# Splitting the sparse-attention indexer's logits into three runs between projection pairs

## What is computed

```python
h = a * jax.nn.sigmoid(gate)                                   # conv group
...
logits = jnp.einsum('bthd,bsd->bths', iqb, ik)                 # 8 indexer heads of width 64
score = jnp.einsum('bths,bth->bts', jax.nn.relu(logits), iwb)  # weighted sum over the heads
score = jnp.where(s_pos <= t_pos, score, -jnp.inf)             # causal
_, idx = lax.top_k(score, topk)                                # topk = 128
```

## Time and profile before

| what | us |
|---|---|
| median of 3 runs | 2079.93 (2078.42 to 2082.22) |
| the profiled execution's own time | 2080.25 |
| its span, from the first to the last instruction | 2078.5 |
| TensorE busy | 2041.9 (98% of the span) |
| VectorE busy | 1325.9 (64%) |
| ScalarE busy | 647.3 (31%) |
| GpSimd busy | 388.3 (19%) |
| mean granted TensorE clock | 0.995 |

### The profile page before, as it was taken

The page is one execution under the profiler, slowest core; times in us unless marked ns, Lnnn a source line. Parts: engine busy times, 40 slices in busy tenths (PEclk is TensorE's granted clock), DMA queues, the critical chain, the costliest instruction groups (busy, mean ns, idle before and its releaser), DMA issues.

```text
span 2078.5 us, 32707 instructions
## 1 busy us (share of the span) xinstructions
PE 2041.9 (98%) x12681; PEld 1813.2 (87%) x12681; DVE 1325.9 (64%) x1891; ACT 647.3 (31%) x1027; POOL 388.3 (19%) x187
## 2 busy tenths in 40 slices
PE   8999999999999899999999999999999999999997
PEld 7778888866888789898999989899998989999896
DVE  1069995364111877675757768576776857677688
ACT  2020000255000154252433425243342524334250
POOL 5536655234556310000000000000000000000010
PEclk9999999999999999999999999999999999999999
DMA  6323343401533234242442423344342333424242
GB/s 198 86 72 90 101 101 99 115 35 41 202 102 102 61 82 132 71 120 85 122 123 82 129 75 109 95 115 123 87 123 82 96 108 103 132 81 126 88 143 81
DMA packets 292039, 214.02 MB, mean 103 GB/s; under 512 B 9510, under 2 KB 256102, under 8 KB 289994
## 3 DMA queue, kind: packets, MB, share of 16 engines
q1 hardware_dynamic: 291834, 211.97, 34.8%
q10 hardware_dynamic: 80, 0.13, 0.0%
HBM read 207.76 MB, written 4.19 MB: 102 GB/s over the span
## 4 chain that ended last, share of the span: by engine, by line
PE 94%; DVE 5%; issue 0%; DMA 0%; ACT 0%; POOL 0%; SPq 0%; DVEq 0%; ACTq 0%
PE psum L1110 13%; PE psum L1106 13%; PE psum L1108 13%; PE psum L1147 7%; PE psum L1148 7%; PE psum L1149 7%; PE psum L736 6%; PE psum L737 6%; PE psum L738 6%; PE psum L967 3%; PE psum L968 3%; PE psum L969 3%; PE psum L947 1%; PE psum L885 1%; DVE acc L1798 1%; DVE acc L1804 1%
## 5 line engine op out<-in xcount | busy, mean ns | idle before, releaser
L1106 PE MATMUL psum<-act,w_room 128*128 128x256 f32 x1344 | 374.7, 279 | 0.0
L1108 PE MATMUL psum<-act,w_room 128*128 128x256 f32 x1344 | 374.7, 279 | 0.0
L1110 PE MATMUL psum<-act,w_room 128*128 128x256 f32 x1344 | 374.7, 279 | 0.0
L1866 DVE TENSOR_TENSOR w_room<-raw,w_room 128x1024 fp32r<-128x1024 f32 x210 | 256.9, 1223 | 128.6 <-ACT w_room L1381 128.6
L1866 DVE TENSOR_TENSOR w_room<-raw_c,w_room 128x1024 fp32r<-128x1024 f32 x164 | 201.0, 1225 | 177.6 <-ACT w_room L1381 177.6
L1381 ACT CAST w_room<-raw 128x1024 fp32r<-128x1024 f32 x212 | 223.4, 1054 | 224.9 <-PE psum L1149 133.0
L1147 PE MATMUL psum<-w_room,h 128*128 128x512 f32 x672 | 262.7, 391 | 2.7 <-DVE h L1896 2.7
L1148 PE MATMUL psum<-w_room,h 128*128 128x512 f32 x672 | 262.0, 390 | 0.0
L1149 PE MATMUL psum<-w_room,h 128*128 128x512 f32 x672 | 261.9, 390 | 0.0
L1108 PEld LDWEIGHTS psum<-act,w_room 128*128 128x128 f32 x1344 | 252.7, 188 | 0.4
L1106 PEld LDWEIGHTS psum<-act,w_room 128*128 128x128 f32 x1344 | 252.7, 188 | 0.4
(11 more groups left out here) (237 smaller groups left out, 3627.5 us busy)
## 6 DMA issues: line engine op xcount, KB each, us to landing
raw_c<-in_w_gate_up SPq DMA_DIRECT2D x84, 512.0 KB, 4.3
raw<-in_w_gate_up SPq DMA_DIRECT2D x84, 512.0 KB, 5.0
raw_c<-in_w_down SPq DMA_DIRECT2D x82, 512.0 KB, 3.8
raw<-in_w_in SPq DMA_DIRECT2D x31, 1024.0 KB, 5.8
raw<-in_w_out SPq DMA_DIRECT2D x16, 1024.0 KB, 5.1
proj<-in_x SPq DMA_DIRECT2D x4, 1024.0 KB, 7.9
acc<-in_x SPq DMA_DIRECT2D x1, 4096.0 KB, 12.5
raw<-in_w_gate_up SPq DMA_DIRECT2D x4, 1024.0 KB, 6.3
```

The lines of the kernel that those rows point to most:

```text
L1106: nc.tensor.matmul(out_ap, stat_hi[:, cols], mov_hi[:, k, :], start=opens and k == 0, stop=False, skip_group_check=not opens)
L1108: nc.tensor.matmul(out_ap, stat_hi[:, cols], mov_lo[:, k, :], start=False, stop=False, skip_group_check=not opens)
L1110: mm = nc.tensor.matmul(out_ap, stat_lo[:, cols], mov_hi[:, k, :], start=False, stop=k == kh - 1, skip_group_check=not opens)
L1866: nc.vector.tensor_tensor(lo, src, hi.bitcast(F32), ALU.subtract).then_inc(lo_ready, 1)
```

## The change

TensorE's order becomes: slabs 5 and 6, the transposes, slabs 7 and 8, the logits of tile 1, slabs 9 and 10, the logits of tile 2, slabs 11 and 12, the logits of tile 3, slabs 13 to 30. ScalarE takes gate 0, the sigmoid of the gates, and then for each tile i `conv_gate(i)` and the eight ReLUs of that tile. VectorE takes value 0 and the head weights, and then for each tile i `conv_value(i)`, the eight score steps and the whole top-k of that tile. No instruction of arithmetic is added or taken away, and the semaphore conditions of each logit, ReLU and score step keep their values.

```diff
-            proj_pairs(N_CONV, 2)
+            proj_pairs(N_CONV, 1)
...
+            def logits(i):
+                for h in range(IDX_HEADS):
+                    e = (i - 1) * IDX_HEADS + h
+                    if e >= 4:
+                        pe.wait_ge(relu_done, e - 3)
...
+            proj_pairs(N_CONV + 2, 1)
             pe.wait_ge(ik_dup, 16)
-            for e in range(3 * IDX_HEADS):
...
-            proj_pairs(N_CONV + 4, 11)
+            logits(1)
+            proj_pairs(N_CONV + 4, 1)
+            logits(2)
+            proj_pairs(N_CONV + 6, 1)
+            logits(3)
+            proj_pairs(N_CONV + 8, 9)
...
+            def positive(i):
+                w = (i + 1) * P
+                for e in range((i - 1) * IDX_HEADS, i * IDX_HEADS):
+                    act.wait_ge(logit_done, e + 1)
+                    if e >= 6:
+                        act.wait_ge(relu_used, e - 5)
+                    nc.scalar.activation(relu_ring[:, e % 6, 0:w], psum[:, 2 + e % 4, 0:w], ACT.Relu)\
+                        .then_inc(relu_done, 1)
+
             conv_gate(0)
-            conv_gate(1)
             act.wait_ge(iwg_ready, 2)
             nc.scalar.activation(iwg[:, :, W_IKW:], iwg[:, :, W_IKW:], ACT.Sigmoid).then_inc(gates_ready, 1)
-            for e in range(3 * IDX_HEADS):
...
-            conv_gate(2)
-            conv_gate(3)
+            for i in range(1, TT):
+                conv_gate(i)
+                positive(i)
...
             conv_value(0)
-            conv_value(1)
...
-            for e in range(3 * IDX_HEADS):
-                i, h = e // IDX_HEADS + 1, e % IDX_HEADS
+            for i in range(1, TT):
+                conv_value(i)
                 w = (i + 1) * P
                 score = sel[:, SEL_OFF[i]:SEL_OFF[i] + w]
...
+                for h in range(IDX_HEADS):
+                    e = (i - 1) * IDX_HEADS + h
...
+                ve.wait_ge(relu_used, i * IDX_HEADS)
                 diagonal = sel[:, SEL_OFF[i] + i * P:SEL_OFF[i] + w]
```

More of the change, by code:

```diff
@@ L815, in _ @@
             mm.then_inc(iwg_t, 1)
-            pe.wait_ge(ik_dup, 16)
-            for e in range(3 * IDX_HEADS):
-                i, h = e // IDX_HEADS + 1, e % IDX_HEADS
[L820 to L825, removed]
-            proj_pairs(N_CONV + 4, 11)
+            def logits(i):
[3 more added lines that the diff above has]
+                        pe.wait_ge(relu_done, e - 3)
+                    half = slice(64 * (h % 2), 64 * (h % 2) + 64)
+                    keys = proj[0:64, S_IKWG, 0:(i + 1) * P] if h % 2 == 0 else ik_high[:, 0:(i + 1) * P]
+                    nc.tensor.matmul(psum[:, 2 + e % 4, 0:(i + 1) * P], proj[half, S_IQ + h // 2, i * P:(i + 1) * P],
+                                     keys, start=True, stop=True).then_inc(logit_done, 1)
+            proj_pairs(N_CONV + 2, 1)
+            pe.wait_ge(ik_dup, 16)
+            logits(1)
[4 more added lines that the diff above has]
+            proj_pairs(N_CONV + 8, 9)
             pe.wait_ge(channel_sum, 1)
@@ L1549, in _ @@
             ve.wait_ge(iwg_ready, 2)
-            for e in range(3 * IDX_HEADS):
-                i, h = e // IDX_HEADS + 1, e % IDX_HEADS
+            for i in range(1, TT):
+                conv_value(i)
                 w = (i + 1) * P
                 score = sel[:, SEL_OFF[i]:SEL_OFF[i] + w]
[L1555 to L1570, removed]
+                for h in range(IDX_HEADS):
+                    e = (i - 1) * IDX_HEADS + h
+                    weight = iwg[:, i, IDX_DIM + h:IDX_DIM + h + 1]
+                    ve.wait_ge(relu_done, e + 1)
+                    if h > 0:
+                        ve.wait_ge(relu_used, e)
+                        nc.vector.scalar_tensor_tensor(out=score, in0=relu_ring[:, e % 6, 0:w], scalar=weight,
+                                                       in1=score, op0=ALU.mult, op1=ALU.add).then_inc(relu_used, 1)
+                    else:
+                        nc.vector.tensor_scalar(score, relu_ring[:, e % 6, 0:w], weight, None, ALU.mult)\
+                            .then_inc(relu_used, 1)
+                ve.wait_ge(relu_used, i * IDX_HEADS)
                 diagonal = sel[:, SEL_OFF[i] + i * P:SEL_OFF[i] + w]
```

## The result

The changed kernel takes 2104.94 us (median of 4 runs, 2103.34 to 2105.37) against 2080.15 for the kernel before on the same chip (4 runs): ratio 1.0118, 95% interval 1.0106 to 1.0131. It is slower by 24.8 us where a gain of 5.8 was forecast. The profiled execution took 2103.34, its span is 2101.5.

A forecast was written before the change was run, and what follows sets the result against it. TensorE was taken as the bound (94% of the chain that ended last). Transposes and logits fall from 16.87 to 11.05 us, a gain of 5.8: 2074.45 from the profiled 2080.25, 2074.1 from the median, stated 2074.3, range 2071.3 to 2078.0.

The forecast's parts named there:

- The sum at the edit: TensorE's transposes and logits between slabs: 0.4 us for transposes plus 2.75, 3.55 and 4.35 for logits, 11.05 against 16.87 before.
- the three runs: TensorE's logits of tiles 1, 2 and 3, 256, 384 and 512 wide, paced by ScalarE's ReLUs: 2.75, 3.55 and 4.35 us.
- Slab 13 was due near 172: Sign of being right: on TensorE, slab 13, the first after the last logits, should start near 172 us.
- the gain should reach the end: Behind L830: TensorE comes 5.8 us earlier, over 20 us of VectorE's wait remain, later work is released by TensorE.
- the gain does not reach the end: Rival, past the edit: some 5 us can be taken back, giving about 2079 to 2080 us; chance 0.07.
- The clock in the runs: TensorE's clock expected at 1.00 from 117 to 180 us; rival of one to three falls, 1.65 us each, chance 0.10.
- The first score step: VectorE, tile 1: asks at about 119.1 during GpSimd's 1.92 us step, through by 120.3 or, missing that, at 124.9.
- the closing steps: VectorE, end of tile 1's top-k: due at about 141 us, with GpSimd idle; `conv_value(2)` follows at 142.6.
- the 6.9: Slack in us at the change's tightest place: `conv_value(3)` done at 176, slab 14 wants the bank at 182.9.
- The rival of a late value: Rival: VectorE late for `conv_value(3)`, so TensorE stalls and the kernel gets slower; chance 0.05.
- its turning point: VectorE's lateness for `conv_value(3)`: TensorE stalls once 6.9 us more are lost; kernel slower than before once 12.7 are.

## Why the prediction was wrong

**The sum at the edit was right.** 0.4 + 2.75 + 3.55 + 4.35 = 11.05; measured for the three runs are 2.71, 3.57 and 4.42. Slab 13 was due near 172 and started at 172.39. The gain at L837 is 5.4 us where 5.8 was worked out. With the layout put right the kernel takes 2073.8, and the forecast was 2074.3.

**The step that failed** is the last one of the costing, "the gain should reach the end". It asked only what the stages behind L830 wait for. It didn't ask what the edit does to the code of the engine that bounds the kernel. The diff shows it: two calls of `proj_pairs` become five, and each is a loop with its own body. The row on which the question hangs was on the page of before, the instruction queue q8. That term stood at nothing; with R = 9 it is 8 x (2.16 + 0.16 + 1.70 x 7/8) = 30.5 us, against a gain of 5.8. Nothing in the trace of before could have given the 3.2 us. The nearest row is q8's packet at 962.56 behind the way back, and it costs nothing there. But the position can be worked out from the compiled program beforehand, and a rival "the hot loop moves to a bad place" would have been fair: by the line, an estimate, some 28 of the 256 places give stops that can be measured.

**The rival "the gain does not reach the end"** put 5 us on what can be taken back. One clock fall did land elsewhere, and by luck in our favour: before, the clock falls at 433 to 436 us, after it doesn't, and the lead grows from 5.4 at L837 to 7.2 at the first `down` matmul. The falls that cost were new ones, behind the stops.

**The clock in the runs** stayed at 1.00 from 75 to 400 us, as said.

**VectorE was wrong in detail.** Its timeline after:

```profile
119.13 1.16 DVE L1573 TENSOR_SCALAR sel<-pt,iwg 128x256 f32<-128x256 f32 x1 [0.25 <-ACT pt L1251]
120.41 8.23 DVE L1570 SCALAR_TENSOR_TENSOR sel<-pt,iwg,sel 128x256 f32<-128x256 f32 x7
...
144.75 0.29 DVE L1583 TENSOR_SCALAR sel<-sel 128x256 f32<-128x256 f32 x1
145.08 4.70 DVE L1584 TENSOR_TENSOR sel<-sel,dist 128x256 f32<-128x256 f32 x1
149.82 0.69 DVE L1548 TENSOR_TENSOR proj<-psum,proj 128x512 f32<-128x512 f32 x1
...
177.26 0.69 DVE L1548 TENSOR_TENSOR proj<-psum,proj 128x512 f32<-128x512 f32 x1
```

and GpSimd's:

```profile
120.23 4.60 POOL L629 TENSOR_TENSOR w_room<-raw,w_room 128x2048 fp32r<-128x2048 f32 x1
...
144.84 4.66 POOL L629 TENSOR_TENSOR w_room<-raw,w_room 128x2048 fp32r<-128x2048 f32 x1
```

The first score step got through, as said. I then took 4.0 us for the other seven, as in the earlier trace rows, but there L629 had just ended. Here it starts at 120.23, 0.18 before them, and they last 8.23: the 4.0 and most of another 4.6. The trace of before had shown such a wait beside L629, 4.05 us, and I had counted it for the first step alone. So the closing steps came at 144.75 instead of 141, met the next L629 and took 4.70, and `conv_value(2)` started at 149.82 instead of 142.6. `conv_value(3)` is 2.0 later than said, at 177.26. Slab 14 wants its bank 10.9 us after 172.39, at 183.3, so a slack of 5.3 us remains of the 6.9. TensorE never waited for it. The rival of a late value was not tested at its turning point; the measured slack says only that it is less far than I thought.

## What to carry to other kernels

An edit that changes how often a loop's body stands in the program moves all code behind it. Look up where the hot loops of the bounding engine start, and keep some 37 instructions (18 matmuls of 0.227 us here) between a loop's start and the end of its 256-instruction block: 24 still left stops here, 37 none. Sixteen transposes of 36x36 ahead of the loop, or one loop more, were worth 31 us here, the edit itself 6. When a profile shows idle time released by "issue" at the same few matmuls of each trip, suspect this first; the cure here was to move the loop, not to undo the edit.

## What the runs showed of the hardware that I had not expected

- A way back whose target lies R instructions before the end of its block (the place of a block's end is set by the stops, not seen) holds TensorE idle for about 3.2 us - 0.113 us x R, 2.9 us at R = 3 and nothing measurable from 37 on, at each trip. In the three trips looked at one packet of instructions moves 2.9 to 3.1 us before the trip's first matmul and the next 0.4 to 0.7 us behind it; in the two with a stop another 2.3 to 2.5 us pass before TensorE goes on.
- The granted clock fell from 1.00 to 0.50 behind a share of these stops that grows with their length: behind 8 of 8 at 2.9 us, 11 of 16 at 2.2 (7 of 8 in one kernel, 4 of 8 in the other), 1 of 8 at 1.8, none at 0.8. Each fall lasts some 3.4 us and gives up half, so a stop of 2.2 us with a fall behind it costs about 4. Why one stop of 2.2 us has a fall behind it and the next has none stays open.
- With sixteen transposes of 36x36 at the start, while TensorE was waiting for loads, the clock read 0.83 from 10 to 20 us in two executions (mean at 369.9 and 371.1) and 1.00 in a third (mean at 368.4).
- A loop of one trip is not free in the program: it stores its body once more, 197 instructions here (R goes from 9 to 68 with one loop more). Straight code and a one-trip loop differ by three (R is 9, 12, 21 and 24 with none, one, four and five loops written straight).
